# Seven block products in place of eight in two down projections

## The reference, cut to what matters

```
D_MODEL = 1024; SEQ = 512; D_FF = 2816
def _swiglu(xn, w_gate, w_up, w_down):
    return (jax.nn.silu(xn @ w_gate) * (xn @ w_up)) @ w_down
...
f = _swiglu(_rmsnorm(h, ffn1_pre_g[i]), ffn1_w_gate[i], ffn1_w_up[i], ffn1_w_down[i])
h = h + 0.5 * _rmsnorm(f, ffn1_post_g[i])
```

## Time and profile before

| | before |
|---|---|
| median of 3 runs | 1556.28 us (1555.72 to 1556.5) |
| span of the profiled execution | 1553.7 us |
| its own time | given as the span alone; the median of the runs is 2.6 us longer |
| instructions | 19027 |
| matmuls, all sizes | 7782 |
| granted TensorE clock | 9 tenths or more in each of 40 slices |
| DMA | 145.12 MB, mean 93 GB/s |

### The profile page before, as it was taken

The page is one execution under the profiler, slowest core; times in us unless marked ns, Lnnn a source line. Parts: engine busy times, 40 slices in busy tenths (PEclk is TensorE's granted clock), DMA queues, the critical chain, the costliest instruction groups (busy, mean ns, idle before and its releaser), DMA issues.

```text
span 1553.7 us, 19027 instructions
## 1 busy us (share of the span) xinstructions
PE 1544.2 (99%) x7782; PEld 1275.7 (82%) x7782; DVE 757.5 (49%) x1193; ACT 595.2 (38%) x956; POOL 155.2 (10%) x162
## 2 busy tenths in 40 slices
PE   9999999999999999999999999999999999999998
PEld 7888888888888888888888888888888877777886
DVE  6444224346546633434843422434647454777645
ACT  6233222335433333323633322233556351544435
POOL 1311000101013400100111100010100010001100
PEclk9999999999999999999999999999999999999999
DMA  5433333322333322333233333333222452121322
GB/s 175 125 95 98 102 99 95 95 95 85 96 92 84 101 86 83 95 96 108 82 95 96 96 99 102 96 95 96 84 86 82 104 112 50 47 55 55 122 82 95
DMA packets 123735, 145.12 MB, mean 93 GB/s; under 512 B 18776, under 2 KB 86496, under 8 KB 123648
## 3 DMA queue, kind: packets, MB, share of 16 engines
q1 hardware_dynamic: 122080, 138.56, 29.6%
q0 software_dynamic: 1568, 5.34, 1.3%
HBM read 141.78 MB, written 2.10 MB: 93 GB/s over the span
## 4 chain that ended last, share of the span: by engine, by line
PE 97%; ACT 1%; DVE 1%; DMA 0%; issue 0%; POOL 0%; POOLq 0%; ACTq 0%
PE G L58 88%; PE X L58 6%; PE X L61 2%; PE G L61 1%; ACT sq_t L64 0%; DMA raw<-in_w_in_dram 0%; ACT whi L64 0%; ACT xh L64 0%; DVE prb L76 0%; ACT prb L64 0%; ACT f L64 0%; DVE xl L73 0%; DVE h L73 0%; ACT post L64 0%; DVE f L70 0%
## 5 line engine op out<-in xcount | busy, mean ns | idle before, releaser
L70 DVE TENSOR_TENSOR wlo<-raw,whi 128x1024 fp32r<-128x1024 f32 (+3 forms) x261 | 313.2, 1209 | 487.0 <-ACT whi L64 486.7
L58 PE MATMUL G<-xh,whi 128*128 128x512 f32 (+1 forms) x1168 | 455.6, 392 | 0.3 <-ACT whi L64 0.3
L58 PE MATMUL G<-xl,whi 128*128 128x512 f32 (+1 forms) x1168 | 449.9, 387 | 0.4 <-DVE xl L73 0.4
L58 PE MATMUL G<-xh,wlo 128*128 128x512 f32 (+1 forms) x1168 | 449.5, 387 | 0.0
L64 ACT ACTIVATE whi<-raw 128x1024 fp32r<-128x1024 f32 (+3 forms) x261 | 266.3, 1031 | 456.0 <-DMA raw<-in_ffn_w_up_dram 160.2
L58 PEld LDWEIGHTS G<-xl,whi 128*128 128x128 f32 x1168 | 219.3, 188 | 45.7 <-DVE xl L73 0.8
L58 PEld LDWEIGHTS G<-xh,whi 128*128 128x128 f32 x1168 | 219.2, 188 | 44.4 <-issue 0.9
L58 PEld LDWEIGHTS G<-xh,wlo 128*128 128x128 f32 x1168 | 219.5, 188 | 42.5 <-DVE wlo L70 0.3
L70 POOL TENSOR_TENSOR tmp_t<-tmp_t,act_t 128x512 f32<-128x512 f32 x52 | 72.3, 1391 | 611.8 <-DVE tmp_t L70 472.6
L58 PE MATMUL G<-whi,ah 128*128 128x512 f32 x320 | 124.6, 389 | 0.0
L58 PE MATMUL G<-whi,al 128*128 128x512 f32 x320 | 124.5, 389 | 0.0
(11 more groups left out here) (272 smaller groups left out, 1792.4 us busy)
## 6 DMA issues: line engine op xcount, KB each, us to landing
raw<-in_w_in_dram SPq DMA_DIRECT2D x55, 512.0 KB, 3.7
raw<-in_ffn_w_gate_dram SPq DMA_DIRECT2D x88, 256.0 KB, 2.8
raw<-in_ffn_w_up_dram SPq DMA_DIRECT2D x88, 256.0 KB, 3.1
raw<-in_ffn_w_down_dram SPq DMA_DIRECT2D x44, 512.0 KB, 3.7
raw<-in_w_in_dram SPq DMA_DIRECT2D x12, 384.0 KB, 3.2
raw<-in_w_out_a_dram SPq DMA_DIRECT2D x8, 512.0 KB, 3.8
raw<-in_w_out_b_dram SPq DMA_DIRECT2D x8, 512.0 KB, 3.7
raw<-in_w_o_dram SPq DMA_DIRECT2D x8, 512.0 KB, 3.8
```

What stands on the lines that cost most here:

```text
L58: return self.e.matmul(out, lhs, rhs, start=start, stop=stop) if self.e else Idle()
L70: return self.e.tensor_tensor(*a) if self.e else Idle()
```

## The change

Behind every three groups of gate and up (6 channel tiles, three pairs) stands one down projection over both column halves and all 512 tokens, called "fast"; three of them take 18 of 22 channel tiles (`PARTS = ((0, 3), (3, 6), (6, 9), (9, 11))`). The last four tiles keep the plain form. For each pair of channel tiles the left matrix is A = [A11 A12; A21 A22] (rows: the two halves of the tokens, 256 each; columns: the two tiles), the right one B (rows: the two tiles, columns: the two halves of the outputs, 512 each). Seven products of blocks stand in place of eight:

- left operands, made once per pair: A11 ("a"), A12 and A22 ("b"), and four sums by GpSimd into `mixr`, 256 elements each: S3 = A11 - A21, S1 = A21 - A22, S2 = S1 - A11, S4 = S2 + A12 ("s"); ScalarE and VectorE split them into `mixh` and `mixl`.
- right operands: down weights lie whole in `near` (pairs 0, 1) and `far` (pair 2), 512 KB per row of 128 channels, loaded by SP during the part's gate/up groups. GpSimd makes sums in place, 512 elements each, one per pair: T1 to T4. A sum may only overwrite a block when its earlier form has been split.
- fourteen steps per part, in a fixed order; a step is the product over pairs 0 and 1 (12 matmuls, 1024 weight columns) or over pair 2 (6 matmuls, 512 columns). ScalarE and VectorE split the weights of every step, and each block again for each product.
- results accumulate in PSUM; P6 goes onto P1's bank after P1 has been taken to `f`, P7 onto P6, P4 onto P7, P3 onto P5. `f` receives 14 additions of 512 columns per part by VectorE (in a first part eight of them are copies by ScalarE).

```diff
+        STEPS = (("P1", (0, 1)), ("P2", (0, 1)), ("P5", (0, 1)), ("P1", (2,)), ("P2", (2,)), ("P5", (2,)),
+                 ("P6", (0, 1)), ("P6", (2,)), ("P3", (0, 1)), ("P7", (0, 1)), ("P7", (2,)), ("P3", (2,)),
+                 ("P4", (0, 1)), ("P4", (2,)))
+        LEFT_OF = {"P1": "a", "P2": "b", "P4": "b", "P5": "s", "P6": "s", "P7": "s", "P3": "s"}
+        SUM_OF = {"P5": "T1", "P6": "T2", "P7": "T3", "P4": "T4"}
...
+            def fast(name, q):
+                banks = {"P1": G[0:2], "P6": G[0:2], "P7": G[0:2], "P4": G[0:2], "P5": G[2:4], "P3": G[2:4], "P2": X[0:2]}
+                onto = {"P6": "P1", "P7": "P6", "P4": "P7", "P3": "P5"}
...
+                for step, (product, pairs) in enumerate(STEPS):
+                    n = first + step
+                    pe.wait_ge(w_lo, n)
+                    for j, p in enumerate(pairs):
...
+                        for t in range(2):
+                            if p == 0 and product in onto:
+                                pe.wait_ge(*freed(name, q, onto[product], t))
...
+                            for wi, tile in ((0, mixh), (1, mixh), (0, mixl)):
...
+                                m = pe.matmul(banks[product][t][:, :], tile[:, p, LEFT[product], t * 128:(t + 1) * 128], w[wi],
+                                              begin, end, product in onto)
```

ScalarE, `split_hi` of such a step, and its order behind the last group of a part:

```diff
+                if n in made:
+                    name, q, product, pairs = made[n]
+                    for p in pairs:
+                        if product in SUM_OF:
+                            act.wait_ge(w_summed, (name, q, SUM_OF[product], p))
+                        else:
+                            act.wait_ge(down_in[p], (name, q))
+                    act.wait_ge(*read_of(n - SLOTS))
+                    act.activation(ring(whi, n), down_source(n), ACT.Copy).then_inc(*w_hi.event(n))
...
+                            left(q, g, "a")
+                            left(q, g, "b")
+                            if g == g1 - 1:
+                                ahead(plan[name, "fast", q][0] + 1)
+                            left(q, g, "s")
```

VectorE, the same order with `left_lo`, and then the steps with the additions to `f` between them:

```diff
+                        for step in range(len(STEPS)):
+                            ahead(plan[name, "fast", q][0] + step)
+                            for after, product, bank in ((4, "P1", G[0:2]), (5, "P2", X[0:2]), (6, "P5", G[2:4]),
+                                                         (8, "P6", G[0:2]), (11, "P7", G[0:2]), (12, "P3", G[2:4])):
+                                if step == after and (q or product in ("P2", "P7", "P3")):
+                                    gather(q, product, bank)
+                        if q:
+                            gather(q, "P4", G[0:2])
```

GpSimd, in each group of a fast part, and behind its last group:

```diff
+                        if q < 3 and g == g1 - 1:
+                            total(q, "T1", 0)
+                            total(q, "T1", 1)
                         for p in range(2):
...
                             pool.tensor_tensor(tmps[slot], tmps[slot], acts[slot], ALU.mult).then_inc(*gated_done.event((name, g, p)))
+                        if q < 3:
+                            left_sums(q, g)
+                    if q < 3:
+                        for into, p in (("T2", 0), ("T2", 1), ("T1", 2), ("T3", 0), ("T3", 1), ("T2", 2), ("T3", 2),
+                                        ("T4", 0), ("T4", 1), ("T4", 2)):
+                            total(q, into, p)
```

SP: `send` skips the steps' units, and behind each of six units of a part's gate/up groups goes one row of the down weights; that of a later part waits for the last step of the part before, that of ffn1's first part for the squares of the input rows (`squared`, "s0", 3), because `far` lies in the buffer `sq_t`:

```diff
+                if q:
+                    sp.wait_ge(*read_of(plan[name, "fast", q - 1][0] + len(STEPS) - 1))
+                elif name == "ffn1":
+                    sp.wait_ge(squared, ("s0", 3))
```

More of the change, by code:

```diff
@@ L55, in wait_ge, with matmul @@
             self.e.wait_ge(signal.sem, signal.at[key])
-    def matmul(self, out, lhs, rhs, start, stop):
-        return self.e.matmul(out, lhs, rhs, start=start, stop=stop) if self.e else Idle()
+    def matmul(self, out, lhs, rhs, start, stop, onto=False):
+        return self.e.matmul(out, lhs, rhs, start=start, stop=stop, skip_group_check=onto) if self.e else Idle()
     def transpose(self, *a):
@@ L248, in two_blocks @@
         cmp_done = signal("cmp_done")
+        down_in, w_summed = [signal(f"down_in{p}") for p in range(3)], signal("w_summed")
         w_hi, x_hi, squared, rooted = signal("w_hi"), signal("x_hi"), signal("squared"), signal("rooted")
@@ L374, in read_of, with in_raw, down_block, down_source @@
             return (w_lo, n) if n in LAST else (acc_done, end_of[n]) if n in end_of else (unit_read, n)
+        def in_raw(n):
+            return n not in made or made[n][2] in IN_RING
+        def down_block(p, product):
+            row, c = RIGHT[product]
+            return near[:, p, row, c:c + 512] if p < 2 else far[row][:, c:c + 512]
+        def down_source(n):
+            _, _, product, pairs = made[n]
+            row, c = RIGHT[product]
+            return near[:, 0:2, row, c:c + 512] if len(pairs) == 2 else far[row][:, c:c + 512]
+        def ring(tile, n):
+            two = len(made[n][3]) == 2
+            return tile[:, n % SLOTS, :].rearrange("p (a c) -> p a c", a=2) if two else tile[:, n % SLOTS, 0:512]
+        def down_lo(n):
+            _, _, product, pairs = made[n]
+            if product in IN_RING:
+                return ring(wlo, n)
+            row, c = RIGHT[product]
+            return near_lo[:, 0:2, row, c:c + 512] if len(pairs) == 2 else far_lo[row][:, c:c + 512]
+        def down_parts(n, j):
+            _, _, product, pairs = made[n]
+            row, c = RIGHT[product]
+            c0 = slice(j * 512, j * 512 + 512)
+            if product in IN_RING:
+                lo = wlo[:, n % SLOTS, c0]
+            else:
+                lo = near_lo[:, pairs[j], row, c:c + 512] if pairs[j] < 2 else far_lo[row][:, c:c + 512]
+            return whi[:, n % SLOTS, c0], lo
+        def unit_of(name, q, product, p):
+            return plan[name, "fast", q][0] + STEPS.index((product, (2,) if p == 2 else (0, 1)))
         def parts_of(n):
@@ L655, in ffn @@
                         g_free[:] = [[(scaled, (name, g, m))] for m in range(4)]
+                    if q < 3:
+                        fast(name, q)
+                        continue
                     for c in range(2):
[L657 to L660, removed]
+                        gemm((name, "dn", c), HT[name], 4, by_token=True, tail=c == 1, hooks=tail_hooks(post, 0) if c else None)
+                        g_free[:] = [[(f_scaled, (name, 1, c, i))] for i in range(4)]
@@ L1904, in ffn @@
                             along(group, 4, ahead, background, pumps if g else (), hooks if g == 0 else None)
+                        if q < 3 and g == g1 - 1:
+                            ahead(plan[name, "fast", q][0])
                         for p in range(2):
@@ L2683, in sync @@
                 send(j)
+                if j in down_after:
+                    send_down(*down_after[j])
                 if j == 8:
```

227 lines of the change are left out of this document (194 added, 33 removed).

## The result

The kernel after takes 1580.07 us (median of 4, 1577.69 to 1580.23) against 1556.39 us for the kernel before on the same chip (median of 4, 1555.72 to 1556.52). The ratio is 1.0149, with a 95% interval of 1.0135 to 1.0163: slower by 23.7 us, where 12.4 were forecast. The profiled spans are 1576.0 and 1553.7 us, 22.3 apart.

What follows compares the result with a forecast made beforehand. TensorE's matmuls were taken to bound the kernel: 24.5 us removed against 36.9 us of new waiting in fast parts, net +12.4 on 1556.3, hence 1568.7 us; range 1541 to 1586, likeliest case 1560 to 1578.

Steps and rivals of the forecast that it cites:

- What is removed: Down projections: 54 fewer matmuls per feed-forward, 108 in all at 0.2267 us, 24.5 us less, 4.08 us per fast part.
- What is added: Fast parts: VectorE weight work 13.4 us and adds 9.7, GpSimd 16.9 at 1.29 per 512-element operation; each fits below 28.56.
- Who blocks whom: Fast parts: every two-input VectorE subtraction and GpSimd sum take turns; waiting 36.9 us with this rule, 10.1 without.
- The walk: Step-by-step timing of one fast part: TensorE waits 6.8 us in four later parts, 4.85 in two first ones, 36.9 in all.
- Edits costed at nothing: Down-weight loads, weight unit 5 sent later by SP, last four tiles, moved scratch tiles, later pool_w load: taken as covered.
- A: Fast parts: GpSimd sums and VectorE subtractions mostly overlap; waits 2.0 and 1.1 us per part, 1541.9 us; chance 0.27.
- C: Fast parts: GpSimd becomes the bound throughout, each sum waiting for a full weight subtraction; near 1587 us; chance 0.14.
- What would show it wrong: Forecast wrong if fast-part gaps are absent, GpSimd operations take about 1.06 us, or TensorE waits for DMA or next group's first units.

Runs made afterwards that it cites:

- e6_all: Kernel after with the edits of e1_masks, e2_rows and e4_early, plus VectorE's adds of P2, P5 and P6 one step earlier: 1534.75 us, ratio 0.9861.
- e4_early: On e1_masks, GpSimd makes T3 and T2 of pairs 0 and 1 before and between the last group's gating multiplies: 1546.3 us, ratio 0.9939.
- e7_writelong: Kernel after with each GpSimd sum replaced by two memsets that read nothing, lengthened to be no shorter than the sums: 1555.12 us, ratio 0.9993.
- e2_rows: Kernel after with SP sending the six down-weight rows of ffn1's first part two units later each: 1574.84 us, ratio 1.012.
- e1_masks: Kernel after with GpSimd building the last masks one background step later, behind the first part's sums: 1573.5 us, ratio 1.0111.

## Why the prediction came out as it did

- **What is removed: right.** 7674 matmuls, 108 fewer; e6_all shows that 24.5 us is their worth, less the 1.0 us of small delays named there.
- **What is added: right in the prices, short in the total.** GpSimd's 1.29 us alone is 1.30 in e4_early's median record; but such sums start 1.25 us apart, not 1.37 as in the walk. GpSimd's busy time grew by 181, not 140 us, since the forecast total held no time in which it is held; the walk did hold that.
- **Who blocks whom: right, and now shown.** With the reads gone and GpSimd's instructions no shorter (e7_writelong), 4.5 of 6.45 us go. The walk without exclusion gave 2.0 and 1.1 us and the kernel without it waits 1.9 and 1.06.
- **The walk: right in place, and in size by two errors that offset each other.** Forecast 36.9 us of waits inside the six parts, measured 36.05; five gaps in a later part, each 0.1 to 0.3 us under its forecast, with 0.1 behind each that the walk did not have; in a first part the 0.4 before step 7 did not come. A step of 1.37 us per sum was 0.12 too long. The forecast's own two walks (6.8 us at 1.29, 5.0 at 1.06) give 7.8 us of waiting per us of price, so 0.12 less is 0.9 less: an estimate of 5.9, where the five gaps add up to 5.84. The 0.6 us behind the gaps made up for two thirds of it, and that is luck. The Trainium skill, "Perfetto Trace Analysis", section "GPSIMD Engine Instruction", asks for start-to-start spacing; the 1.41 that the forecast took for it was read from reductions with collisions in them and gave 7.1 us a later part. The spacing of sums that nothing holds is 1.25, so here the page's method, on such a row, comes nearest, and the recorded 1.29 is 0.04 off.
- **Edits costed at nothing: this step had it wrong**, by 9.0 us (6.24 + 2.80) of the 11.3 between forecast and result, in two of its sentences. "Moved scratch tiles and the later pool_w load stand behind work of 300 us" looked at when their results are needed, not at what is queued behind them. GpSimd's mask step was in the kernel before too, and there stood ahead of nothing urgent; the change put T1 behind it: 6.24 us. And "it lands by 30.2 and is split 2.3 us later, which leaves 5 us" counted cover up to the use of unit 5. Its second half was issued at 27.39 instead of about 26.5 and it landed at 32.0, 1.8 us later than figured from a landing time of another stage, with DMA at 0.71 in place of the earlier trace rows's 0.30. But even on its own numbers the cover ended earlier: the evictions of the group before stand behind its low half on VectorE. Of the 2.8 us, 1.8 are the late landing and, by this estimate, 1.0 would have come without it; e2_rows shows that the whole goes when unit 5 is sent early again. The rest of the 11.3 is 0.8 us at the start less as much in the walk (36.9 - 36.05), the 0.9 behind the last fast parts, where the forecast counted on full cover, and 1.4 between the medians' difference and the spans' (23.7 - 22.3).
- **Rivals.** A (1541.9) would have needed no exclusion: the kernel without it ran at 1555.1 with the holes in it. C (1587) is not what happened, though the total came near: its walk waits 10.1 us in a later part and 7.6 in a first one, and no part exceeds 6.7. Its total was reached by the two holes, which no rival had.
- **What would show it wrong** named "if TensorE waits for a DMA". It never does; in the second hole it waits for an eviction behind a split behind a DMA. The view of waits named `act_t`, and only VectorE's timeline showed what stood ahead of it.

## What to carry to other kernels

Before work moves to an idle engine, list what on it and on VectorE reads two SBUF tiles, and place the moved work where VectorE has time to be held: the order of GpSimd's sums alone, with the same instructions, was worth 4.4 us of 35 in each later part. Count cover up to the first urgent thing queued behind an instruction on its in-order engine, not up to the use of its own result; and before an urgent job is given to an engine with background work, look up what that work waits for.

## What the runs showed of the hardware

I had not expected holes of about the same length to differ in what follows them. In the kernel after, 2.80 us without a matmul left the granted clock of the stretch at 1.00 (2.4 GHz). In e4_early 2.73 us at the same place, and in e1_masks 4.09, were followed by some 3.3 us at the lower level, 0.50 (1.2 GHz): 15 x 0.11 / 0.50, by the windows from 30 to 45 us of these two kernels:

```profile
30.00:45.00 15.00, 12.43 (x49) 9.84 (x48) 7.70 (x11) 7.02 (x9) 7.47 (x8) 0.89 0.60 202
```

```profile
30.00:45.00 15.00, 11.07 (x43) 8.65 (x42) 6.38 (x9) 5.70 (x8) 7.09 (x8) 0.89 0.57 194
```

In the kernel after, the clock fell towards the end of the 6.24 us without a matmul and was low for 6.8 us in all (20 x 0.17 / 0.50, by its window from 75 to 95 us above):

```profile
87.00:88.00 1.00, 0.77 (x2) 0.71 (x3) 1.00 (x3) 0.63 (x1) 0.17 (x1) 0.50 0.00 0
...
94.00:96.00 2.00, 2.00 (x11) 1.62 (x10) 0.56 (x1) 1.58 (x2) 2.00 (x3) 1.00 0.00 0
```

At 0.50 a matmul takes 0.427 us from start to start in place of 0.2267, and 13 of them cost 2.6 us. Yet the part's excess is only 0.5 us above the 4.96 it has in e1_masks: while TensorE was slower the late sums caught up. In e1_masks the part waits 1.10 and 1.44 us before P2 and P5 of pair 2, here 0 and 0.41, so 2.1 us of the loss came out of later waits. What decides between a hole that lowers the clock and one that doesn't stays open.
